# Second block's output projection, layer norms, modulation, residual and tail, token-major in tiles of 128 tokens

## The chip, the cores and the metric

One NeuronCore of a Trainium2 chip (trn2) runs the whole program. Five engines work on their own instruction streams and meet at semaphores: PE multiplies matrices, DVE and ACT work element by element, POOL does small vector work and indirect transfers, SP issues most transfers. The metric is the device time of one execution in microseconds, as the median of several runs.

## The reference

A model of two blocks on 512 tokens of width 1024, float32. The change lies in the second block. Cut to what matters:

```python
def _layernorm(z, gain=None, bias=None):
    mu = mean(z); var = mean(square(z - mu))
    y = (z - mu) * rsqrt(var + 1e-6)
    return y if gain is None else y * gain + bias

def _modulate(z, shift, scale):
    return _layernorm(z) * (1 + scale) + shift

mod = silu(c) @ w_ada + b_ada                      # 6 rows of 1024: sh1 sc1 g1 sh2 sc2 g2
mixed = _mixer(...)                                # mLSTM heads and RWKV heads, 512 + 512 wide
x = _layernorm(ALPHA * x + g1 * (mixed @ w_out), ln1_g, ln1_b)
ffn = _hier_moe(_modulate(x, sh2, sc2), ...)       # 32 experts, 2 chosen for each token
x = _layernorm(ALPHA * x + g2 * ffn, ln2_g, ln2_b) # the output
```

The routing takes logits = h @ rt + bias with h the modulated activation, 36 of them for each token (4 groups, 32 experts), picks a group and two experts in it, and weights their results by `share`.

## The kernel before

Activations lie feature-major: a tensor `[128, 8, 512]` holds feature k*128+p of token t at partition p, chunk k, column t. Weights stream from memory in units of `[128, 2048]` (1 MB, sixteen 128x128 blocks) through a ring of four buffers; `Weights.feed` on SP reloads a buffer when `w.used` says it is free, and the last reloads of a stage already bring the next stage's units.

`rwkv_stage` (L2056) runs the RWKV scan in six steps of 128 tokens in two directions. SP loads the factors F of step p into one of two buffers when step p-2 is through with it (L2126); no other transfer follows the masks of step 0.

`route_stage` (L2696) comes next. `HeadNorm` (L2558) normalises the RWKV heads of the mixer output `o` in place: PE sums, DVE centres, ACT squares, PE sums squares, a reciprocal on DVE, then four `tensor_spread` matmuls that DVE multiplies in, chunk by chunk. Between these PE works ahead on the output projection (`chunk`, L2747): output chunk m of 128 features is one PSUM bank of 512 tokens, eight matmuls with a 128x128 weight block stationary and a chunk of `o` moving; chunks 0 to 4 take their first four k early. DVE then adds the gated product to `x`, which ACT has multiplied by ALPHA (L2818, L2903). Then `Norm` (L2641) runs twice, first with ln1's gain and bias in place, then with the modulation into `h`: eight ones-matmuls give the mean over features to every partition (`sum_chunk`, L2658), DVE subtracts it (L2681), ACT squares (L2671), eight ones-matmuls sum the squares (L2663), DVE, ACT and DVE make the 128x512 rstd (L2684, L2673, L2686), DVE multiplies (L2690) and ACT applies scale and shift (L2676). PE then makes the logits with `rt` stationary (36 rows, 512 columns; L2779), turns them to token-major (L2783), and turns `h` into `tokens_sb`, 128 tokens at a time (L2790, ACT copies L2913), which SP stores to `tokens` in memory (L2736). DVE meanwhile does the routing from L2828 on; PE gives it ranks (L2796, L2799) and the slot table (L2805).

`experts_stage` (L2927) loops over 32 experts: POOL gathers token rows by slot from `tokens`, PE multiplies, POOL scatters results to `pair_rows`; SP feeds the ring. `tail_stage` (L3195) loads the two result rows of each token in four tiles, DVE scales and sums them (L3228, L3230), PE turns each tile to feature-major (L3244), DVE adds gate times it to `x` (L3235), and a third `Norm` runs; each of its eight chunks is stored to `out` as it is placed (L3215).

The order on each engine is written out by hand; stages are blocks with a barrier between them.

## Time and profile before

| | us |
|---|---|
| median of 3 runs (3359.12 to 3368.25) | 3359.33 |
| the profiled execution's own time | 3374.72 |
| its span, first to last instruction | 3372.9 |
| PE busy | 3055.4 (91%) |
| DVE busy | 1942.2 (58%) |
| ACT busy | 1274.9 (38%) |
| POOL busy | 909.9 (27%) |
| mean granted TensorE clock | 0.957 of 2.4 GHz |

Busy times are sums over the span, so an engine with 91% can still leave whole stretches to others; a stretch is read from the windows. A granted clock of 1.0 is 2.4 GHz and 0.5 is 1.2 GHz. A matmul of float32 operands stands in the trace as two records.

### The profile page before, as it was taken

What the parts mean: (1) busy time and instruction counts of PE and PEld (TensorE: products, weight loads), DVE (VectorE), ACT (ScalarE), POOL (GpSimd) and SP (SyncE); (2) the same over time, 40 slices, a digit from 0 to 9 for tenths busy, and PEclk for the clock granted to TensorE, in tenths of its full rate; (3) what the DMA queues carried; (4) which work ended last, traced back from release to release, by engine and by line L of the source; (5) the groups of instructions that cost most, each with busy time, mean ns of one, the idle gap of its engine ahead of it and who ended that gap; (6) DMA issues with size and microseconds to landing.
All of it is one profiled execution on the core that took longest, in us unless ns stands there. A gap on an engine that the chain in (4) does not pass through costs nothing. (4 is left out here: it accounts for less than half of the span.)

```text
span 3372.9 us, 54470 instructions
## 1 busy us (share of the span) xinstructions
PE 3055.4 (91%) x22376; PEld 2398.5 (71%) x22376; DVE 1942.2 (58%) x2706; ACT 1274.9 (38%) x1607; POOL 909.9 (27%) x468
## 2 busy tenths in 40 slices
PE   7989999998999979999989998369999769999995
PEld 5567888797777757888768777257785358888783
DVE  3656552201433335563299837865653469999895
ACT  2544322222333333322232222412222247787773
POOL 3023444333222204344312210000100024454431
PEclk9989999999999989999999998779999979999997
DMA  3633222322111103222221100411102159999994
GB/s 143 231 120 112 95 92 100 132 88 77 61 63 57 57 29 109 89 98 97 104 75 63 50 18 1 149 63 43 39 29 92 38 213 354 362 384 364 361 368 195
DMA packets 77474, 439.69 MB, mean 130 GB/s; under 512 B 14944, under 2 KB 18016, under 8 KB 28512
## 3 DMA queue, kind: packets, MB, share of 16 engines
q1 hardware_dynamic: 67776, 427.38, 34.2%
q0 software_dynamic: 9504, 9.47, 0.8%
q8 instruction: 153, 2.51, 0.3%
q14 instruction: 41, 0.34, 0.0%
HBM read 422.11 MB, written 39.85 MB: 137 GB/s over the span
## 5 line engine op out<-in xcount | busy, mean ns | idle before, releaser
L77 POOL TENSOR_TENSOR ring_lo<-ring,unit_hi 128x2048 fp32r<-128x2048 f32 x116 | 536.6, 4626 | 1124.0 <-ACT unit_hi L72 1124.0
L130 PE MATMUL wide<-h_hi,unit_hi 128*128 128x512 f32 x1296 | 516.0, 398 | 44.8 <-DVE h_lo L191 23.3
L132 PE MATMUL wide<-h_hi,ring_lo 128*128 128x512 f32 x1296 | 516.8, 399 | 0.0
L131 PE MATMUL wide<-h_lo,unit_hi 128*128 128x512 f32 x1296 | 515.7, 398 | 0.0
L3149 DVE TENSOR_TENSOR ex_w_lo<-ring,ex_w_hi 128x2048 fp32r<-128x2048 f32 x192 | 437.7, 2288 | 49.5 <-ACT ex_w_hi L3099 48.8
L3099 ACT CAST ex_w_hi<-ring 128x2048 fp32r<-128x2048 f32 x192 | 365.9, 1908 | 123.3 <-DMA ring<-in_weights 115.6
L72 ACT CAST unit_hi<-ring 128x2048 fp32r<-128x2048 f32 x116 | 220.5, 1901 | 417.8 <-PE wide L132 416.3
L130 PEld LDWEIGHTS wide<-h_hi,unit_hi 128*128 128x128 f32 x1296 | 249.7, 193 | 116.4 <-POOL ring_lo L77 18.8
L131 PEld LDWEIGHTS wide<-h_lo,unit_hi 128*128 128x128 f32 x1296 | 245.7, 190 | 53.6 <-issue 0.2
L132 PEld LDWEIGHTS wide<-h_hi,ring_lo 128*128 128x128 f32 x1296 | 245.1, 189 | 52.4
L362 DVE TENSOR_TENSOR ffn_hidden_lo<-ffn_whole,ffn_hidden_hi 128x512 f32 (+1 forms) x44 | 201.0, 4568 | 51.6 <-ACT ffn_hidden_hi L337 51.6
L3042 PE MATMUL wide<-ex_w_hi,ex_x_hi 128*128 128x512 f32 x512 | 204.9, 400 | 7.5 <-DVE ex_x_lo L3154 6.2
L3044 PE MATMUL wide<-ex_w_hi,ex_x_lo 128*128 128x512 f32 x512 | 201.5, 394 | 0.0
L3043 PE MATMUL wide<-ex_w_lo,ex_x_hi 128*128 128x512 f32 x512 | 201.1, 393 | 0.0
L3001 POOL TENSOR_TENSOR ex_held<-ex_blank 128x1 f32<-128x1 f32 x64 | 90.1, 1407 | 320.8 <-DVE ex_results L3178 319.6
L130 PE MATMUL wide<-in_hi,in_unit_hi 128*128 128x512 f32 (+3 forms) x424 | 148.3, 350 | 16.1 <-DVE in_lo L1207 8.8
L1480 DVE SCALAR_TENSOR_TENSOR conv<-grid,cols,conv 128x512 f32<-128x512 f32 x160 | 158.4, 990 | 3.5
L132 PE MATMUL wide<-in_hi,ring_lo 128*128 128x512 f32 (+3 forms) x424 | 147.1, 347 | 0.0
L2514 ACT COPY rw_Q<-wide 128x256 f32<-128x256 f32 (+1 forms) x144 | 53.5, 371 | 230.6 <-PE wide L2217 189.9
L130 PE MATMUL wide<-ffn_hidden_hi,unit_hi 128*128 128x512 f32 x352 | 140.1, 398 | 0.0
L131 PE MATMUL wide<-ffn_hidden_lo,unit_hi 128*128 128x512 f32 x352 | 139.7, 397 | 0.0
L132 PE MATMUL wide<-ffn_hidden_hi,ring_lo 128*128 128x512 f32 x352 | 138.0, 392 | 0.0
(526 smaller groups left out, 6006.9 us busy)
## 6 DMA issues: line engine op xcount, KB each, us to landing
ring<-in_weights SPq DMA_DIRECT2D x356, 1024.0 KB
factors<-rp_out SPq DMA_DIRECT2D x8, 1536.0 KB, 5.5
rw_F<-factors SPq DMA_DIRECT2D x12, 1024.0 KB
tail_both<-pair_rows_out SPq DMA_DIRECT2D x4, 1024.0 KB, 7.9
x<-in_x SPq DMA_DIRECT2D x1, 2048.0 KB, 7.5
x_kept<-x SPq DMA_DIRECT2D x1, 2048.0 KB, 11.9
x<-x_kept SPq DMA_DIRECT2D x1, 2048.0 KB
x_mixing<-x SPq DMA_DIRECT2D x1, 2048.0 KB, 7.3
```

Source lines behind the costliest of these rows:

```text
L72: act.copy(self.hi[n % 2][:, :], self.ring[n % RING][:, :]).then_inc(self.hi_ready, 1)
L77: pool.tensor_tensor(self.lo[n % RING][:, :], self.ring[n % RING][:, :], self.hi[n % 2][:, :].bitcast(F32), ALU.subtract).then_inc(self.lo ...
L130: pe.matmul(dst, a[0], b[0], start=start, stop=False)
L131: pe.matmul(dst, a[0], b[1], start=False, stop=False)
L132: return pe.matmul(dst, a[1], b[0], start=False, stop=stop)
L362: dve.tensor_tensor(hidden[1][:, j * RING + i, :], whole[:, i % 2, :], hidden[0][:, j * RING + i, :].bitcast(F32), ALU.subtract).then_inc( ...
L1480: dve.scalar_tensor_tensor(out=go, in0=shifted(dy, dx), scalar=weight(dy, dx), in1=go, op0=ALU.mult, op1=ALU.add).then_inc(convolved, 1)
L3042: pe.matmul(dst, a_hi, b_hi, start=first, stop=False)
L3043: pe.matmul(dst, a_hi, b_lo, start=False, stop=False)
L3044: return pe.matmul(dst, a_lo, b_hi, start=False, stop=last)
L3099: act.copy(w_hi[at % RING][:, :], w.ring[n % RING][:, :]).then_inc(hi_ready, 1)
L3149: dve.tensor_tensor(w_lo[at % RING][:, :], w.ring[n % RING][:, :], w_hi[at % RING][:, :].bitcast(F32), ALU.subtract).then_inc(w.used, 1)
```

## The change

- The weight units of `w_out` are laid out by row chunk, so unit n holds k = 2n and 2n+1 for all 1024 outputs. A tile of the projection is 128 tokens by 1024 features in two banks: `o`'s 128x128 block is stationary and 512 weight columns move.
- `x` (feature-major, from memory) is turned on PE in eight rounds of four transposes through bank 5; ACT multiplies by ALPHA on the way into `normed`.
- Gate, gains, biases, scale and shift are needed along the free dimension. Four modulation vectors are stored to `mod_rows` in memory during `rwkv_stage` (step 2, SP), and they and `ln_rows` are loaded into all 128 partitions: five in `route_stage`, three at the start of `experts_stage`.
- `Norm` is replaced by `RowNorm`: for each tile of 128 tokens two `bn_stats`, one `bn_aggr`, and the norm as two `scalar_tensor_tensor` around a square root and a reciprocal of one column.
- The modulated tile is already what goes to `tokens`; it is turned (eight transposes, two ACT copies) only for the logits, which come out token-major with the bias added on DVE.
- The tail works on the tiles as they are loaded and stores four tiles; ACT takes over the first product with `share`. PE has nothing to do there.

The diff's core:

```diff
 rwkv_stage, sync:
+                    if p == 2:
+                        for to, of in stores:
+                            sp.dma_start(to, of, allow_slow_non_contiguous=True).then_inc(rows_stored, 16)
+                sp.wait_ge(rows_stored, 16 * len(stores))
...
+class RowNorm:
+    def vector(self, dve, n, src, mid, dst, scale, shift):
+        for i in range(2):
+            self.step(dve.bn_stats(self.parts[:, i, :], src[:, i * T:(i + 1) * T]), i == 1)
+        dve.bn_aggr(self.stats[:, n, :], self.parts[:, :, :].rearrange("p i s -> p (i s)")).then_inc(self.measured, 1)
+        dve.wait_ge(self.measured, n + 1)
+        dve.scalar_tensor_tensor(out=mid, in0=src, scalar=self.stats[:, n, 0:1], in1=scale, op0=ALU.subtract, op1=ALU.mult)
+        dve.wait_ge(self.root_ready, n + 1)
+        self.step(dve.reciprocal(self.rstd[:, n:n + 1], self.rstd[:, n:n + 1]))
+        return dve.scalar_tensor_tensor(out=dst, in0=mid, scalar=self.rstd[:, n:n + 1], in1=shift, op0=ALU.mult, op1=ALU.add)
+    def scalar(self, act, n):
+        act.wait_ge(self.measured, n + 1)
+        act.activation(self.rstd[:, n:n + 1], self.stats[:, n, 1:2], ACT.Sqrt, bias=self.eps[:, 0:1]).then_inc(self.root_ready, 1)
...
 route_stage, sync:
-                for n in range(RING):
+                for n in range(2):
                     w.load(sp, w.at + n)
                 sp.dma_start(x[:, :, :], kept).then_inc(head.x_back, 16)
+                for n in range(2, RING):
+                    w.load(sp, w.at + n)
...
 route_stage, tensor:
+                def tile(t, halves, first_k, last_k):
+                    for k in range(first_k, last_k):
+                        if k >= MC:
+                            pe.wait_ge(head.mixed_ready, k - MC + 1)
+                        unit = w.arrived(pe, 0, k // 2)
+                        for half in halves:
+                            b = k % 2 * D + half * T
+                            mm = pe.matmul(c.bank[2 * t + half][:, :], o[:, k, t * P:(t + 1) * P], unit[:, b:b + T], start=(k == 0), stop=(k == DC - 1))
+                        if t == TT - 1 and k % 2 == 1:
+                            mm.then_inc(w.used, 1)
+                    return mm
                 head.tensor_sums(pe)
-                chunk(0, 0, MC)
+                tile(0, (0, 1), 0, MC)
                 head.tensor_squares(pe)
-                chunk(1, 0, MC)
-                chunk(2, 0, MC)
+                tile(1, (0, 1), 0, MC)
                 head.tensor_spread(pe, 0)
                 head.tensor_spread(pe, 1)
-                chunk(3, 0, MC)
+                for n in range(4):
+                    turn_x(n // 2, n % 2)
                 head.tensor_spread(pe, 2)
                 head.tensor_spread(pe, 3)
...
+                for n in range(4, 2 * TT):
+                    turn_x(n // 2, n % 2)
+                tile(2, (0,), 0, MC)
+                for t in range(2):
+                    tile(t, (0, 1), MC, DC).then_inc(tile_done, 1)
+                tile(2, (0,), MC, DC)
+                pe.wait_ge(x_grown, 2 * TT)
+                tile(2, (1,), 0, DC).then_inc(tile_done, 1)
+                pe.wait_ge(head.scaled, MC)
+                tile(3, (0, 1), 0, DC)
+                turn_h(0)
+                turn_h(1)
+                logits_of(0)
+                turn_h(2)
+                logits_of(1)
+                logits_of(2)
+                turn_h(3)
+                logits_of(3)
...
 route_stage, vector, for each tile t:
+                    for half in range(2):
+                        cols = slice(half * T, (half + 1) * T)
+                        dve.tensor_tensor(h[:, t, cols], c.bank[2 * t + half], rows.gate[:, cols], ALU.mult).then_inc(gated, 1)
+                    dve.tensor_tensor(normed[:, t, :], normed[:, t, :], h[:, t, :], ALU.add).then_inc(added, 1)
+                    norm.vector(dve, 2 * t, normed[:, t, :], normed[:, t, :], normed[:, t, :], rows.scale1, rows.shift1).then_inc(normed_ready, 1)
+                    norm.vector(dve, 2 * t + 1, normed[:, t, :], h[:, t, :], h[:, t, :], rows.scale2, rows.shift2).then_inc(tokens_ready, 1)
...
 experts_stage, sync:
+                for to, of in rows_of:
+                    sp.dma_start(to, of).then_inc(rows_loaded, 16)
...
 tail_stage, scalar:
+                for t in range(TT):
+                    act.wait_ge(loaded[t], 16)
+                    act.mul(both[:, t, 0, :], both[:, t, 0, :], route.share[:, t, 0:1]).then_inc(scaled, 1)
+                    norm.scalar(act, t)
 tail_stage, vector, for each tile t (waits left out):
+                    dve.scalar_tensor_tensor(out=y, in0=both[:, t, 1, :], scalar=route.share[:, t, 1:2], in1=y, op0=ALU.mult, op1=ALU.add).then_inc(summed, 1)
+                    dve.tensor_tensor(y, y, rows.gate, ALU.mult).then_inc(gated, 1)
+                    dve.tensor_tensor(x[:, t, :], x[:, t, :], y, ALU.add).then_inc(added, 1)
+                    norm.vector(dve, t, x[:, t, :], x[:, t, :], x[:, t, :], rows.scale, rows.shift).then_inc(placed, 1)
...
+                stores = [(mod_rows[n].rearrange("(k p) -> p k", p=P), source[:, part * DC:(part + 1) * DC, 0])
+                          for n, source, part in ((GATE1, mod, 2), (SHIFT2, mod, 3), (SCALE2, mod1, 4), (GATE2, mod, 5))]
```

## Rows read from the trace of the kernel before

**Rows 1.** Windows: us, busy and (count) of PE, PEld, DVE, ACT, POOL, granted clock, DMA share, GB/s
```profile
2643.00:2668.00 25.00, 17.15 (x32) 6.34 (x32) 13.83 (x18) 11.39 (x17) 0.00 (x0) 0.86 0.08 34
2668.00:2696.00 28.00, 19.12 (x46) 6.03 (x45) 14.88 (x21) 12.68 (x18) 0.00 (x0) 0.88 0.00 1
2696.00:2719.00 23.00, 13.22 (x75) 11.04 (x73) 14.45 (x74) 4.23 (x7) 0.00 (x0) 0.78 0.23 91
2719.00:2731.00 12.00, 0.82 (x4) 0.82 (x5) 4.49 (x2) 5.01 (x4) 9.54 (x17) 0.52 0.64 232
2731.00:3325.00 594.00, 575.98 (x2686) 474.93 (x2684) 520.33 (x318) 437.24 (x318) 253.64 (x242) 0.98 0.93 350
3325.00:3372.90 47.90, 23.42 (x64) 12.22 (x64) 27.33 (x34) 16.93 (x26) 0.00 (x0) 0.71 0.33 132
```

**Rows 2.** Timeline, norm stretch: start us, us, engine, line, out<-in, idle before
```profile
2643.46 4.88 DVE L2681 SCALAR_TENSOR_TENSOR x<-wide,x 128x512 f32<-128x512 f32 x8 [1.82 <-PE wide L2658]
...
2653.99 3.35 DVE L2686 RECIPROCAL norm_rstd<-norm_rstd 128x512 f32<-128x512 f32 x1 [0.70 <-ACT norm_rstd L2673]
...
2695.73 0.31 DVE L2828 COPY rt_L<-wide 128x144 f32<-128x144 f32 x1 [1.17 <-PE wide L2783]
```

**Rows 3.** Timeline, PE in the output projection
```profile
2575.03 5.40 PE L2747 MATMUL wide<-late,ring 128*128 128x512 f32 x8 [2.13 <-DMA ring<-in_weights]
...
2595.20 13.90 PE L2747 MATMUL wide<-late,ring 128*128 128x512 f32 x32
```

**Rows 4.** Timeline, PE's first token transposes
```profile
2695.62 1.97 PE L2790 MATMUL wide<-ident,h 128*128 128x128 f32 x16
```

**Rows 5.** Groups by shape, DVE: line, names, shapes, count | busy us, mean ns | idle before
```profile
L1943 DVE TENSOR_TENSOR_SCAN rp_cum<-rp_reset,rp_sg 128x768 f32<-128x768 f32 x4 | 7.0, 1757 | 2.8 <-ACT rp_up L1891 1.9 <-ACT rp_sg L1876 0.9
...
L3230 DVE SCALAR_TENSOR_TENSOR tail_both<-tail_both,share 128x1024 f32<-128x1024 f32 x4 | 5.1, 1284 | 0.1
...
L3228 DVE TENSOR_SCALAR tail_both<-tail_both,share 128x1024 f32<-128x1024 f32 x4 | 3.0, 754 | 13.8 <-DMA tail_both<-pair_rows_out 13.8
...
L1707 DVE RECIPROCAL ml_small<-ml_small 128x4 f32<-128x4 f32 x16 | 2.9, 178 | 0.6
...
L2619 DVE TENSOR_TENSOR late<-late,wide 128x512 f32<-128x512 f32 x4 | 2.7, 684 | 2.3 <-PE wide L2599 2.3
...
L2880 DVE TENSOR_TENSOR rt_at_high<-iota,rt_high 128x1024 f32<-128x1024 f32 x1 | 1.2, 1225 | 0.0
...
L2606 DVE COPY hn_heads<-ident 128x512 f32<-128x512 f32 x1 | 0.4, 418 | 0.0
```

**Rows 6.** Groups by shape, ACT
```profile
L2527 ACT COPY rw_base<-wide 128x512 f32<-128x512 f32 x1 | 0.6, 586 | 0.2 <-PE wide L2288 0.2
```

**Rows 7.** Timeline, tail: first product, last transposes, DVE's first read, stores
```profile
3330.63 0.75 DVE L3228 TENSOR_SCALAR tail_both<-tail_both,share 128x1024 f32<-128x1024 f32 x1 [12.60 <-DMA tail_both<-pair_rows_out]
...
3340.18 1.97 PE L3244 MATMUL wide<-ident,tail_both 128*128 128x128 f32 x8 [0.50 <-DVE tail_both L3230]
3340.70 5.36 DVE L3235 SCALAR_TENSOR_TENSOR x<-wide,mod,x 128x512 f32<-128x512 f32 x8 [0.57 <-PE wide L3244]
...
3365.62 5.26 SPq L3215 DMA_DIRECT2D out<-x  x8
```

**Rows 8.** Windows, PE just after the second norm's sums may start
```profile
2658.00:2664.00 6.00, 5.03 (x6) 2.19 (x7) 4.29 (x8) 5.75 (x8) 0.00 (x0) 0.50 0.00 0
```

**Rows 9.** F loads on SP, their first matmuls by line, page's part 3
```profile
2304.95 0.32 SPq L2126 DMA_DIRECT2D rw_F<-factors  x1
...
2356.33 2.49 SPq L2126 DMA_DIRECT2D rw_F<-factors  x2
...
L2180 PE MATMUL wide<-rw_F x64: 212/218/268, 2363.5 to 2367.6; 64*64 64x64 f32 x64
...
q1 hardware_dynamic: 67776, 427.38, 34.2%
q0 software_dynamic: 9504, 9.47, 0.8%
```

More of the change, by code:

```diff
@@ L2693, with route_stage @@
 NOBODY = 1 << 20
-def route_stage(nc, c, w, o, x, kept, g, bonus, gate, first, second, h, consts, loads, route, tokens):
+def route_stage(nc, c, w, o, x, kept, g, bonus, rows, hT, consts, loads, route, tokens):
     NR = E_GROUPS + EXPERTS
@@ new lines, in logits_of @@
+                def logits_of(t):
+                    if t == 0:
+                        pe.wait_ge(gated, 2 * 2)
+                        pe.wait_ge(loaded, 16 * len(loads))
+                    for k in range(DC):
+                        if k % 4 == 0:
+                            pe.wait_ge(h_copied, 2 * t + k // 4 + 1)
+                        mm = pe.matmul(logits[:, t * NR:(t + 1) * NR], hT[:, t % 2, k, :], rt[:, k, :], start=(k == 0), stop=(k == DC - 1))
+                    mm.then_inc(logits_done, 1)
@@ L2762, in _ @@
-                for m in range(DC):
-                    chunk(m, MC if m < head.EARLY else 0, DC)
-                    if m >= 2:
-                        pe.wait_ge(added, m - 1)
-                        first.sum_chunk(pe, m - 2)
-                for k in range(DC - 2, DC):
-                    pe.wait_ge(added, k + 1)
-                    first.sum_chunk(pe, k)
-                first.sum_squares(pe)
-                for k in range(DC):
-                    pe.wait_ge(first.placed, k + 1)
-                    second.sum_chunk(pe, k)
@@ L2775, in _ @@
-                second.sum_squares(pe)
-                pe.wait_ge(loaded, 16 * len(loads))
-                for k in range(DC):
-                    pe.wait_ge(second.placed, k + 1)
-                    mm = pe.matmul(logits, rt[:, k, :], h[:, k, :], start=(k == 0), stop=(k == DC - 1))
-                mm.then_inc(logits_done, 1)
-                pe.wait_ge(logits_copied, 1)
-                for t in range(TT):
-                    mm = pe.matmul(small[:, t * NR:(t + 1) * NR], LT[:, t * P:(t + 1) * P], c.ident[0:NR, 0:NR], start=True, stop=True)
@@ L2811, in _ @@
                 head.vector(dve)
-                for m in range(DC):
-                    if m % 2 == 0:
-                        dve.wait_ge(chunk_done, m // 2 + 1)
-                    else:
-                        dve.wait_ge(w.used, w.at + m // 2 + 1)
-                    dve.wait_ge(grown, m + 1)
-                    dve.scalar_tensor_tensor(out=x[:, m, :], in0=c.bank[m][:, :], scalar=gate(m), in1=x[:, m, :],
-                                             op0=ALU.mult, op1=ALU.add).then_inc(added, 1)
@@ L3192, in experts_stage, with tail_stage @@
     w.at += ALL
-def tail_stage(nc, c, route, pair_rows, x, gate, scale, shift, out):
+def tail_stage(nc, c, route, pair_rows, rows, rows_loaded, out):
     with ExitStack() as ctx:
@@ L3224, in _ @@
             @block.vector
             def _(dve):
+                norm.begin(dve)
                 for t in range(TT):
[L3227 to L3228 removed]
+                    y = both[:, t, 0, :]
                     dve.wait_ge(scaled, t + 1)
[L3230 to L3231 removed]
@@ L3368, in second_block @@
-            second = Norm(c, x, dev, h, at(4, 0, True), at(3), c.bank[2], c.bank[3], squares, rstd[:, 1, :])
-            loads = [(rt[:, :, :], a["rt"]), (rt_bias[:, :], a["rt_bias"]), (iota[:, :], a["iota"]), (earlier[:, :], a["earlier"]),
-                     (pairs[:, :, :, :], a["pairs"])]
-            route_stage(nc, c, w, mixed, x, kept, r.g, r.bonus, at(2), first, second, h, (rt, rt_bias, iota, earlier, pairs), loads, route, tokens)
-        experts_stage(nc, c, w, route, tokens, pair_rows)
+            hT, rows = late[:, 8192:8192 + 2 * D].rearrange("p (i k t) -> p i k t", i=2, t=P), Bag()
@@ new lines, in second_block @@
+            route_stage(nc, c, w, mixed, x, kept, r.g, r.bonus, rows, hT, (rt, rt_bias, iota, earlier, pairs), loads, route, tokens)
+        rows, rows_loaded = Bag(), nc.alloc_semaphore("tail_rows_loaded")
+        rows.gate, rows.scale, rows.shift = [sb(f"tail_row_{n}", [P, D])[:, :] for n in ("g2", "ln2_g", "ln2_b")]
+        rows_of = [(rows.gate, mod_rows[GATE2].partition_broadcast(P)), (rows.scale, a["ln_rows"][2].partition_broadcast(P)),
+                   (rows.shift, a["ln_rows"][3].partition_broadcast(P))]
```

251 lines of the change are left out of this document (114 added, 137 removed).

## The prediction

> **What bounds the kernel now.** I read the stretches first [rows 1]. The expert stretch, 594 of 3372.9 us, keeps the DMA queues busy 0.93 of the time at 350 GB/s; the change touches nothing in it. What it touches lies in two places where one engine after another works alone. From 2643 to 2696 us the two layer norms run feature-major over the whole 1024 x 512 activation: PE is busy 17.15 of 25 us and 19.12 of 28 us, DVE and ACT 11 to 15 us each. The timeline shows the relay [rows 2]: centring may start only when all eight chunk sums are in (2643.46), the rstd needs all eight squares, the reciprocal of a 128x512 tile costs 3.35 us (2653.99), the second norm repeats all of it, and the logits and their turn follow. So 52.3 us pass between the first centring (2643.46) and the first routing instruction on the copied logits (L2828, 2695.73). The tail, 3325 to 3372.9, is the same relay once more, with PE at clock 0.71. Routing itself (2696 to 2719) is small DVE instructions, which stay.
>
> **Part 1: PE up to the first finished tile.** The projection is 64 f32 matmuls of 512 moving columns in either layout. Sixteen took 13.90 us (32 records), so 0.86 to 0.87 each [rows 3]; token-major swaps which operand is stationary and keeps count and columns. I take no gain or loss. The start is as before: the first unit lands at 2575.03 and the first four matmuls take 5.40 us there. Now eight stand before the head norm's squares: 5.4 + 4 x 0.86 = 8.9, to 2583.9. Squares (1.0) and tile 1's eight (6.9) go to 2591.8, two spreads to 2593.5. Then come the added turns of x: eight rounds of four transposes on PE and one ACT multiply into SBUF, through a single bank, so a relay. Sixteen transposes took 1.97 us [rows 4], 0.12 each; DVE's first read in the tail began 0.52 us after its transposes did [rows 7]; an ACT copy of 128x512 out of PSUM is 0.59 [rows 6]. One round is 0.52 + 3 x 0.12 + 0.59 + 0.05 = 1.5 us, eight are 12.2, and two more spreads stand between them (1.7): 2607.4. Twelve matmuls follow before tile 0 is whole (half of tile 2's first four chunks, then tile 0's last four): 10.3, so 2617.7. After a stretch in which PE had idled and then worked in bits, the granted clock was 0.50 [rows 8]; the turns are such bits. All turns at half rate would add 3 us and the first matmuls behind them 2.5. I add 0.8, giving 2618.5, and keep 0 and 5.5 as ends.
>
> **Part 2: DVE per tile, route stage.** Now DVE carries both norms alone, tile by tile. Prices are from [rows 5]: two gate products out of PSUM, 0.684 each, 1.37; residual add, 128x1024, 1.225. One norm: two bn_stats of 128x512, one aggregate on 12 values (0.18, as small ones take), two scalar_tensor_tensor of 128x1024 at 1.284, a reciprocal of one column 0.178. No bn_stats is in this trace. As a one-pass instruction it costs about what a tensor_tensor of that width does, 0.684; that is my value, being an elementwise read with no second operand. Its lower end is the SBUF copy, 0.418; its upper end the scan's two cycles an element, 1757 ns for 768, so 1.17. The norm is then 1.37 + 0.18 + 2.57 + 0.18 = 4.30. A tile is 1.37 + 1.23 + 8.60 + 0.4 for some fourteen gaps of 0.03 = 11.6 us, and four are 46.4. ACT's square root of one column (about 0.2 us) lies under the scalar_tensor_tensor of 1.284 that stands between it and its reader. PE needs 6.9, 10.3 and 13.8 us for tiles 1, 2 and 3, together 31.0, while DVE works 34.8 on three tiles: DVE waits only for tile 0, and PE has 3.8 us of cover. DVE ends at 2618.5 + 46.4 = 2664.9. Behind the last tile stand eight transposes (the clock low by then, 0.246 each), a pair of ACT copies of which one is exposed, and the last four small logits matmuls: 1.3 + 1.0 + 0.6 + 1.2, to 2669.0 against 2695.73. That is 26.7 us. Removed with it: LT's copy, the logits' transposes, the token transposes and their copies; the last two lay beside routing and give nothing. But they kept PE at work just ahead of the rank matmuls. These and the sixteen records of L2805 will find a low clock; routing ran at 0.78 on average [rows 1], and going to 0.5 on about 6 us of its matmuls costs about 1.5. Route: 25.2 us.
>
> **Part 3: queues.** On SP, x is asked for behind two units instead of four and the loads grow by five rows spread over 128 partitions, 2.5 MB. In all 9 MB from 2569 at 350 to 430 GB/s are in by 2595, and the first reader is DVE at 2618: covered by 23 us. The refill with expert weights, which waited for the early chunks, now waits for tile 3 (2635 to 2648); 4 MB land by 2660, and the experts start about 2693: covered. The token stores stand behind these waits on SP and are needed only then. In the RWKV stage SP gets four stores whose elements are 4 bytes: 4096 packets, issued about 2305.3, behind one tile's F loads and ahead of the next F load (2356.33) on the same queue; that tile's first matmul starts at 2363.5 [rows 9], about when its 2 MB are in, so there is no lead to spend. Nothing in the trace writes 4-byte pieces to memory from a tile. The software queue's packets, of 1 KB in the mean, took 0.8% of 16 x 3372.9 over 9504, 0.045 us each; all of q1's took 0.27. So the stores are through after 12 us, or after 69. I take the low value, since 4 bytes are nearer to 1 KB than to q1's 6.3, and count nothing. The experts' queue gets 1.5 MB of rows before its first weight: 4 us at 350 GB/s in a stretch that used the DMA 0.64 [rows 1], sharing with the gather PE waits for. I count 0.7 lost; 0 to 4 are the ends.
>
> The Trainium skill (DMA: Bandwidth & Descriptors, Rules for kernel authors) says that a strided last dim is lowered to one descriptor per element and should be made contiguous; the same page puts read-modify-write under 512 B. It speaks against these stores. By it the packets are slow, and the sum would lose what rival C loses; no row here shows a 4-byte store.
>
> **Part 4: tail.** Tile 0's pair rows are in at 3330.63 [rows 7]. ACT scales them (1.0, from 0.586 for half the width, less one start [rows 6]), a product DVE had made in 0.754 [rows 5]; DVE then does 1.284 (sum), 1.225 (gate), 1.225 (add) and a norm of 4.30, with gaps 8.35. Four are 33.4: 3331.6 + 33.4 = 3365.0. ACT's next scaling (1.0) runs beside the last two DVE steps. The loads came every 2.5 us and are no longer the bound. The last store is 512 KB instead of 256 KB; the last one was issued at about 3370.6 and the span ended 2.3 later, so I give 3.1: 3368.1. Gain 4.8 us. Gone are 16 ones-matmuls, 32 transposes and the 3.35 reciprocal.
>
> **The sum.** 25.2 + 4.8 - 0.7 = 29.3. The profiled execution's own time was 3374.7 (span 3372.9), so 3345.4 there. The runs' median was 3359.3, 15.4 lower than that execution; the shortened parts do not depend on it, so 3359.3 - 29.3 = 3330.0.
>
> **Rivals.**
> (B) bn_stats takes two cycles an element, like the scan: 24 x (1.17 - 0.684) = 11.7 us back, 3341.7. For: it keeps a mean and a variance. Against: nothing chained to the previous element has to be waited for.
> (B2) bn_stats streams at the SBUF copy's rate, 24 x 0.27 = 6.4 more: 3323.6. DVE's three tiles then take 31.6 us, still over PE's 31.0, so all of it shows. VectorE: DVE Perf Modes of the Trainium skill (Mode 2x_2P) has single-source f32 operations in SBUF at two elements a cycle; the trace agrees for tensor_scalar, 754 against 1284 ns [rows 5], but the page leaves open which operations have it.
> (C) The 4-byte stores hold the queue. With q1's mean of 0.27 us a packet they last 69 us from 2305.3, to 2374.4, so F for the next tile starts 18 us late and PE stands as long: 3348.
> (D) The same, slower than before. If a packet takes t us, the stores end at 2305.3 + 256 t, and PE waits 256 t - 51. It equals my gain at t = 0.31. At 0.35 us it is 38.6 against 29.3: 3368.6. For: single elements and a destination in memory. Against: t would be over q1's mean, whose packets hold 427.38 MB / 67776 = 6.3 KB, where q0's of 1 KB took 0.045.
> (E) The norms gain, but PE with its turns and low clock becomes the bound instead of DVE: the full 5.5 us where 0.8 is counted, and another 3.5 at tile 3, 8.2 in all: 3338.
>
> **How the numbers follow.** Forecast (3325 to 3336) 0.58, B 0.12, B2 0.07, C 0.06, D 0.06, E 0.11. The predicted time is the forecast's, 3330.0. The range 3316 to 3348 takes in B, B2, E and the nearer half of C; left out are D, the rest of C, and of the others the part that their own spread puts beyond it, together under 0.2. A change of 0.3% is 10 us, about what a measurement of this kernel can tell from none. Faster: forecast, B, B2 and E, 0.88, less 0.01 for several losses at once: 0.87. Same: C, which at 3348 stands on the edge of 0.3%, and that 0.01: 0.07. Slower: D, 0.06.
>
> **What would show it.** The bn_stats row near 0.68 us; DVE's tiles 11.6 us apart with no wait for PE after the first; first gate product at 2618; logits added at 2669; DVE in the tail 8.35 a tile, out stores at intervals; 4096 4-byte packets over well before 2356, and no long PE wait on rw_F. Wrong would be a PE wait on rw_F of tens of us, a bn_stats over 1.2, or gate products waiting for tile 1 or 2.

## The result and the profile after

| | us |
|---|---|
| median of the changed kernel, 4 runs (3327.13 to 3332.01) | 3330.0 |
| median of the kernel before beside it, 4 runs (3359.12 to 3370.02) | 3363.79 |
| ratio, with its 95% interval | 0.9892 (0.9875 to 0.9909) |
| span of the profiled execution, before | 3372.9 |
| span of the profiled execution, after | 3327.9 |

The time came out at 3330.0 us, the forecast's own figure. That is less of a success than it looks: the stretches below show two terms of 9 and 17 us, of opposite sign, that the forecast had at zero. First the page of the changed kernel, its busy times and two of its DMA queues; q1 has 4880 packets more than before for 4.2 MB more [rows 9].

```profile
PE 2990.6 (90%) x22320; PEld 2383.9 (72%) x22320; DVE 1954.2 (59%) x2725; ACT 1250.8 (38%) x1572; POOL 898.5 (27%) x468
...
q1 hardware_dynamic: 72656, 431.59, 35.1%
...
q8 instruction: 153, 2.51, 0.3%
```

Windows of the kernel after, columns as in [rows 1]. In order: route stage to the first gate product; to the last token row finished; to the logits added; routing; experts up to PE's first transposes; the rest of the experts; the tail.

```profile
2561.10:2606.60 45.50, 39.45 (x113) 17.69 (x114) 17.74 (x25) 10.37 (x17) 0.00 (x0) 0.96 0.52 203
2606.60:2650.70 44.10, 39.04 (x144) 21.65 (x142) 42.84 (x60) 5.37 (x14) 0.00 (x0) 0.95 0.38 132
2650.70:2656.30 5.60, 5.42 (x24) 5.06 (x24) 0.09 (x2) 2.45 (x3) 0.00 (x0) 0.50 0.23 94
2656.30:2682.80 26.50, 12.92 (x44) 11.16 (x44) 14.69 (x74) 0.52 (x3) 0.00 (x0) 0.55 0.00 0
2682.80:2696.80 14.00, 0.00 (x0) 0.00 (x0) 4.53 (x3) 5.09 (x4) 10.76 (x19) 0.53 0.95 334
2696.80:3286.00 589.20, 572.63 (x2688) 474.39 (x2688) 520.42 (x318) 437.94 (x319) 243.59 (x240) 0.99 0.94 353
3286.00:3327.90 41.90, 0.00 (x0) 0.00 (x0) 31.28 (x37) 10.60 (x13) 0.00 (x0) 0.50 0.38 151
```

DVE is busy 42.84 of the 44.10 us in which the four tiles are made: it is the bound there, where before [rows 1, 2] three engines took turns. One tile on DVE's timeline; the first row's 11.53 us is the only wait for PE's products, and the next tile begins at 2617.61 with none:

```profile
2606.59 1.29 DVE L2838 TENSOR_TENSOR tokens_sb<-wide,row_g 128x512 f32<-128x512 f32 x2 [11.53 <-PE wide L2737]
...
2607.91 1.22 DVE L2841 TENSOR_TENSOR y<-y,tokens_sb 128x1024 f32<-128x1024 f32 x1
...
2609.17 1.29 DVE L2663 BATCH_NORM_STATS2 rt_norm_parts<-y 128x6 f32<-128x512 f32 x2
...
2610.49 0.21 DVE L2664 BATCH_NORM_AGGREGATE rt_norm_stats<-rt_norm_parts 128x2 f32<-128x12 f32 x1
...
2610.73 1.29 DVE L2666 SCALAR_TENSOR_TENSOR y<-y,rt_norm_stats,row_ln_g 128x1024 f32<-128x1024 f32 x1
...
2616.41 1.29 DVE L2669 SCALAR_TENSOR_TENSOR tokens_sb<-tokens_sb,rt_norm_rstd,row_sh 128x1024 f32<-128x1024 f32 x1
...
2617.61 1.28 DVE L2838 TENSOR_TENSOR tokens_sb<-wide,row_g 128x512 f32<-128x512 f32 x2
```

PE over the same stage: the products ahead of the squares, the turns of x as a relay with ACT (1.34 us a round), the 96 records behind them without a gap, and the last tile's logits and the slots with the clock at 0.50 to 0.55.

```profile
2566.89 8.83 PE L2737 MATMUL wide<-ring,late 128*128 128x512 f32 x16 [1.86 <-DMA ring<-in_weights]
...
2586.62 0.66 PE L2752 MATMUL wide<-ident,x 128*128 128x128 f32 x4 [0.69 <-ACT y L2924]
2587.96 0.66 PE L2752 MATMUL wide<-ident,x 128*128 128x128 f32 x4 [0.69 <-ACT y L2924]
...
2595.98 41.37 PE L2737 MATMUL wide<-ring,late 128*128 128x512 f32 x96
...
2652.59 3.63 PE L2776 MATMUL wide<-rt,late 128*128 128x36 f32 x16
...
2674.15 6.74 PE L2822 MATMUL wide<-rt_named,rt_at_low 128*128 128x256 f32 x16 [5.86 <-DVE rt_named L2905]
2696.81 1.97 PE L3072 MATMUL wide<-ident,tokens_sb 128*128 128x128 f32 x8 [15.93 <-DMA tokens_sb<-tokens,ex_take]
```

**Where the time went.** The program falls into stretches by the start of one instruction each: the first load of RWKV factors (L2126), SP's first instruction of the route stage, of the experts, of the tail. The difference of the two spans is 45.0 us, and these are all of it:

| stretch | before | after | difference | forecast |
|---|---|---|---|---|
| all up to the first RWKV factors | 2191.7 | 2175.0 | -16.7 | 0 |
| RWKV stage | 377.3 | 386.1 | +8.8 | 0 |
| route stage | 149.9 | 121.7 | -28.2 | -25.2 |
| experts (of it up to PE's first transposes) | 606.9 (11.3) | 603.2 (14.0) | -3.7 (+2.7) | +0.7 |
| tail | 47.1 | 41.9 | -5.2 | -4.8 |

The execution of before that was profiled took 3374.7 us, 11 over its median, and that of after 3329.7, which is its median; so 34 us is what runs show, and the table's parts are 11 us richer than that. No instruction of the first row's stretch was changed. The experiments are about that row and the second.

### The profile page after: what moved, and what is told of

Same layout as the page of the kernel before. It is cut to its first block and busy times, and to the rows that moved or that the text cites. A ratio compares the mean times of both kernels' runs of the same rounds, so it can differ in the third digit from the quotient of the medians.

```text
span 3327.9 us, 54357 instructions
## 1 busy us (share of the span) xinstructions
PE 2990.6 (90%) x22320; PEld 2383.9 (72%) x22320; DVE 1954.2 (59%) x2725; ACT 1250.8 (38%) x1572; POOL 898.5 (27%) x468
## 3 DMA queue, kind: packets, MB, share of 16 engines
q8 instruction: 153, 2.51, 0.3%
## 5 line engine op out<-in xcount | busy, mean ns | idle before, releaser
L130 PE MATMUL wide<-h_hi,unit_hi 128*128 128x512 f32 x1296 | 516.1, 398 | 44.9 <-DVE h_lo L191 23.0
L132 PE MATMUL wide<-h_hi,ring_lo 128*128 128x512 f32 x1296 | 508.1, 392 | 0.0
L131 PE MATMUL wide<-h_lo,unit_hi 128*128 128x512 f32 x1296 | 507.9, 392 | 0.0
L130 PEld LDWEIGHTS wide<-h_hi,unit_hi 128*128 128x128 f32 x1296 | 245.2, 189 | 110.6 <-POOL ring_lo L77 18.8
L130 PE MATMUL wide<-in_hi,in_unit_hi 128*128 128x512 f32 (+3 forms) x424 | 149.5, 353 | 15.0 <-DVE in_lo L1207 8.0
L130 PE MATMUL wide<-ffn_hidden_hi,unit_hi 128*128 128x512 f32 x352 | 139.1, 395 | 0.0
```

The lines of the kernel that those rows point to most:

```text
L130: pe.matmul(dst, a[0], b[0], start=start, stop=False)
L131: pe.matmul(dst, a[0], b[1], start=False, stop=False)
L132: return pe.matmul(dst, a[1], b[0], start=False, stop=stop)
```

## The experiments

Of each kernel one execution was profiled. Stretches as in the table above; "gate" is route start to the first gate product, "logits" from there to the logits added, "routing" from there to the experts. The first row is the kernel before, unedited; its medians are those of the four sets of its runs that stood beside the others.

| kernel | median us (runs) | ratio to before, 95% | up to RWKV | RWKV | gate | logits | routing | first transposes | experts | tail |
|---|---|---|---|---|---|---|---|---|---|---|
| before | 3363.79 to 3366.93 | 1 | 2191.7 | 377.3 | 33.3 | 93.4 | 23.2 | 11.3 | 606.9 | 47.1 |
| after_again | 3332.24 (4) | 0.9896 (0.9864 to 0.9929) | 2179.4 | 384.3 | 43.7 | 49.8 | 25.6 | 13.2 | 606.5 | 42.0 |
| bn_twice | 3344.67 (7) | 0.9937 (0.9918 to 0.9956) | 2169.8 | 381.4 | 45.5 | 59.2 | 24.9 | 13.2 | 603.8 | 46.5 |
| before_no_recip | 3355.36 (10) | 0.9973 (0.9958 to 0.9988) | 2190.0 | 371.7 | 31.1 | 87.4 | 23.1 | 11.5 | 606.2 | 45.3 |
| tile0_first | 3326.73 (4) | 0.9886 (0.9864 to 0.9909) | 2176.8 | 380.5 | 41.9 | 50.9 | 25.3 | 14.5 | 609.4 | 42.1 |
| warm_route | 3326.10 (4) | 0.9889 (0.9868 to 0.9909) | 2171.9 | 381.2 | 45.4 | 48.4 | 23.0 | 14.5 | 610.9 | 42.0 |
| rows_at_end | 3326.49 (4) | 0.9883 (0.9848 to 0.9917) | 2177.1 | 382.1 | 43.6 | 49.7 | 26.0 | 11.3 | 606.7 | 42.1 |
| no_stores | 3906.40 (4) | 1.1604 (1.1567 to 1.1641) | 2174.4 | 369.9 | 47.2 | 49.7 | 26.0 | 14.0 | 1195.9 | 42.1 |
| stores_x5 | 3369.24 (10) | 1.0006 (0.9994 to 1.0018) | 2179.1 | 421.7 | 47.3 | 49.7 | 25.8 | 14.9 | 606.4 | 42.2 |
| rows_by_pe | 3320.31 (4) | 0.9857 (0.9836 to 0.9877) | 2176.9 | 372.8 | 46.7 | 49.7 | 25.8 | 13.5 | 611.5 | 41.9 |
| cols_padded | 3344.41 (4) | 0.9927 (0.9908 to 0.9946) | 2195.2 | 385.9 | 43.4 | 49.7 | 25.9 | 13.5 | 609.5 | 42.0 |
| before_narrow | 3349.34 (6) | 0.9945 (0.9927 to 0.9963) | 2175.5 | 373.2 | 31.5 | 92.7 | 23.0 | 11.3 | 610.3 | 47.0 |
| best | 3311.94 (4) | 0.9843 (0.9827 to 0.9859) | 2170.6 | 376.0 | 40.8 | 48.8 | 20.5 | 14.1 | 609.1 | 42.2 |

**after_again**: the changed kernel once more, unedited.

> The changed kernel itself, unaltered, for what its stages do from run to run. Theory 1 (the added RWKV time of its profile, 386 us against 377, is the clock's own wandering): the stretch from the first F load to the first out-projection weight load comes out between 377 and 386 and the granted clock in step 2 of it differs from the first profile's 0.84. Theory 2 (the 4-byte stores bring the clock down): again about 386 with a clock near 0.84 in step 2. Route stage 121 to 122 us, tail 42 us in either.

3332.24 us. It shows how far one kernel's stretches vary from execution to execution: 4.4 us up to RWKV, 1.8 at the gate, 3.3 in the experts.

### Is DVE's tile the bound, and what does the norm cost?

**bn_twice**: every bn_stats is issued twice, the first into a spare tile.

```
+ self.step(dve.bn_stats(self.parts2[:, n, i, :], src[:, i * T:(i + 1) * T]), False)
  self.step(dve.bn_stats(self.parts[:, i, :], src[:, i * T:(i + 1) * T]), i == 1)
```

> Every bn_stats issued twice, the first into a tile nobody reads. Theory 1 (DVE is the bound of both places and PE stays covered): 24 more at about 0.65 us each add 15.5 us in all, 10.3 in the route stage and 5.2 in the tail. Theory 2 (PE or the relay of waits is the bound in the route stage): under 5 us more there, 5.2 in the tail.

The groups of DVE by shape in this kernel, the real ones and the added ones of the route stage:

```profile
L2664 DVE BATCH_NORM_STATS2 rt_norm_parts<-y 128x6 f32<-128x512 f32 x16 | 11.0, 686 | 0.3
L2665 DVE BATCH_NORM_STATS2 rt_norm_parts<-y 128x6 f32<-128x512 f32 x16 | 10.8, 676 | 0.0
```

Sixteen added instructions of 0.676 us are 10.8 us; the stretch "logits" grew by 9.5 (49.7 to 59.2). Eight in the tail are 5.4; the tail grew by 4.5. Nearly all of what DVE is given shows up in the time, in both stages: DVE is the bound, and an instruction saved there is worth its duration.

**before_no_recip**: the kernel before with the reciprocal of the 128x512 tile (3.35 us [rows 2]) replaced by a copy; the three norms leave out the reciprocal, so their outputs are others.

```
- dve.reciprocal(self.rstd, self.rstd).then_inc(self.rstd_ready, 1)
+ dve.tensor_copy(self.rstd, self.rstd).then_inc(self.rstd_ready, 1)
```

> The kernel before, in which the three layer norms copy the 128x512 root instead of taking its reciprocal (the reciprocal is left out, so the output is not the reference's). Theory (the norms of before are a relay and every instruction of it is on the path): 3 x (3.35 - 0.42) = 8.8 us less than before. Rival (another engine's work fills in): under 3 us less.

In the route the two norms gave back 6.0 us (93.4 to 87.4) where two times 3.35 - 0.43 are 5.8, the tail 1.8 of 2.9. So the reciprocals are some 8 of the 33 us that route and tail gained; the other 25 lie in the rest of the relay, which the token-major form ends as well.

### The route's smaller terms

**tile0_first**: the third tile's first products no longer stand ahead of the first two tiles' last ones.

```
- tile(2, (0,), 0, MC)
  for t in range(2):
      tile(t, (0, 1), MC, DC).then_inc(tile_done, 1)
- tile(2, (0,), MC, DC)
+ tile(2, (0,), 0, DC)
```

> The four early matmuls of tile 2 stand behind tiles 0 and 1 instead of ahead of tile 0's last ones. PE's total is unchanged. Theory (DVE bound with 2.45 us of cover for PE at tile 3): first gate product 3.4 us earlier, DVE then waits about 1.1 us for PE at tile 3, and the route stage is 2.3 us shorter. Rival (PE is as much a bound): DVE waits more at tiles 2 or 3, and the stage is 0 to 1 us shorter.

The first gate product came 41.9 us after the route's start in place of 43.7 and 45.5 (43.4 to 47.3 in the nine profiles with the old order), and 1.1 to 1.2 of that was lost again behind it, where DVE now waits once more for PE's products (1.1 us). The route is 118.1 us against 119.1 and 121.7; the median, 3326.73, cannot be told from that of after.

**warm_route**: four matmuls without use ahead of the last tile's transposes, six behind its logits and ahead of the wait for the ranks' input, six behind the ranks.

```
+ warm(4)          # four times pe.matmul(c.bank[3], c.ones, o[:, 0, :])
  turn_h(3)
  logits_of(3)
+ warm(6)
  ...
  mm.then_inc(ranks_done, 1)
+ warm(6)
```

> Adds 16 matmuls whose result nobody reads, in three gaps of PE: four before the last tile's transposes, six before the ranks, six before the slot table. Theory (the route's end lost time because PE stood idle and its granted clock fell to 0.53 there): the clock in that stretch above 0.8, last logits 3.6 to under 2.5, ranks 6.3 to 3.5, slot table 6.7 to 3.5 us, and the route stage 5 to 8 us shorter. Rival (the added matmuls end too late or the rate is set by other things): gain under 2 us or a loss of up to 3.

"Logits" 48.4 in place of 49.7, routing 23.0 in place of 25.6 and 26.5: 4 to 5 us of what the low clock of the two windows after 2650.7 above costs; it was still 0.85 in this kernel's routing. The total moved by less than its spread.

**rows_at_end**: the tail's rows are asked for behind the last expert weight, not ahead of the first.

```
- for to, of in rows_of:                      # ahead of the ring
-     sp.dma_start(to, of).then_inc(rows_loaded, 16)
  ... all of the experts' weights ...
+ for to, of in rows_of:
+     sp.dma_start(to, of).then_inc(rows_loaded, 16)
```

> The three rows for the tail are loaded behind the experts' last weight unit instead of ahead of the first. Theory 1 (they delayed the first gather, for which PE waits): from the experts' first DVE instruction to PE's first transpose 11.3 us instead of 14.0, and the whole 2.7 us shorter. Rival (the stage is bound by the weight transfers, so the gather's delay is made up): 11.3 us likewise, the total the same as the changed kernel.

PE's first transposes come after 11.3 us, as before the change, in place of 13.2 and 14.0: those 2 to 3 us are the rows. But the expert stretch as a whole takes 606.7, with 606.5 and 603.2 where the start is late. Over all profiles but that of no_stores it is 606.2 to 610.3 us (mean 607.5) in the four that start early, and 603.2 to 611.5 (607.8) in the nine that start late. That fits a stretch in which the DMA, at 0.93 of its time, sets the end and a late first expert is made up; but 2 us would not stand out of this spread, so it is not shown. Nor does the median tell: 3326.49 is 3.5 and 5.8 us under the two of after, and the single times overlap.

### The four stores

**no_stores**: the four stores left out, and other rows of the same size loaded where their results were read. The modulation is then another, the tokens fall to the experts otherwise, and the loop over the experts runs twice; only its stretches ahead of the experts are read.

```
- rwkv_stage(..., stores)
+ rwkv_stage(..., [])
- (rows.gate, mod_rows[GATE1].partition_broadcast(P))
+ (rows.gate, a["ln_rows"][0].partition_broadcast(P))
```

> Leaves out the four 4-byte stores of the modulation vectors; gate, scale and shift rows are loaded from the layer-norm rows instead, so the output is not the reference's. Theory 1 (stores cost nothing): same total as the changed kernel within 0.1%, RWKV stretch anywhere in 377 to 386. Theory 2 (the stores slow the RWKV stage through the clock or the queue): RWKV stretch back to 377 in the profile and the total 6 to 9 us lower than the changed kernel.

**stores_x5**: the four stores and sixteen more like them into a tensor that nothing reads.

```
+ stores += [(extra_rows[4 * i + n].rearrange("(k p) -> p k", p=P), of) for i in range(4) for n, (to, of) in enumerate(stores[:4])]
```

> The same four 4-byte stores and sixteen more like them into other memory rows, 20480 packets in place of 4096. The forecast's mechanism (a queue before the next F load, free while it is short): the four took about 15 us from their issue, so twenty take about 75 and end 12 to 21 us after the next F load was due; PE waits on rw_F by that much and the total is 3342 to 3351 us. Rival (packets of 4 bytes pass beside other loads): no added PE wait on rw_F, total as the changed kernel's.

No stores: the RWKV stage takes 369.9 us. Five times the stores: 421.7, and 37 us on the median, all of the change's gain and more than either theory gave it. In both PE waits 36 us for rw_F, as in after (36.8): it is the first load's landing, and the factors behind the stores are never late. So the queue that the forecast looked at is not what makes it slow. Windows of 10 us around the stores; in after they are issued from 2287.26 on. First after, then no_stores, then 40 us of stores_x5 (the DMA share goes over 1 there because the records of small packets overlap):

```profile
2285.00:2295.00 10.00, 6.94 (x226) 6.34 (x226) 4.58 (x12) 1.12 (x3) 0.00 (x0) 0.81 0.72 204
2295.00:2305.00 10.00, 5.10 (x88) 4.24 (x89) 1.43 (x4) 0.37 (x1) 0.00 (x0) 0.50 0.21 2
2305.00:2315.00 10.00, 9.43 (x189) 7.05 (x191) 5.52 (x13) 1.12 (x3) 0.95 (x3) 0.67 0.01 2
```

```profile
2285.00:2295.00 10.00, 7.02 (x280) 6.26 (x275) 4.49 (x12) 1.86 (x5) 0.00 (x0) 1.00 0.60 214
2295.00:2305.00 10.00, 9.21 (x306) 7.38 (x307) 8.32 (x19) 1.49 (x4) 1.58 (x4) 1.00 0.02 5
2305.00:2315.00 10.00, 9.87 (x183) 7.35 (x181) 9.71 (x20) 1.84 (x5) 2.74 (x6) 1.00 0.01 2
```

```profile
2298.00:2338.00 40.00, 28.95 (x438) 21.77 (x435) 12.30 (x28) 2.23 (x6) 1.72 (x5) 0.54 1.15 3
```

In the ten microseconds from 2295 all engines do little in after (PE 88 matmuls in place of 306, DVE 4 instructions in place of 19), and the clock is 0.50 where it stays at 1.00 without the stores. What DVE waits for, in after, and last what L2416 waits for in the whole stage (us, times, longest):

```profile
2293.00 0.44 DVE L2416 COPY_PREDICATED rw_X<-level_mask,wide 128x256 f32<-128x256 uint32 x1 [0.23 <-PE wide L2246]
...
2302.24 0.45 DVE L2416 COPY_PREDICATED rw_X<-level_mask,wide 128x256 f32<-128x256 uint32 x1 [8.47 <-remote]
...
DVE rw_X L2416 <- PE wide L2246: 119.0, 78, 4.6
```

"Remote" is the profile's word for a signal that it can put down to no instruction just before it. The semaphore that L2416 waits for is raised by PE's matmuls of L2246; here that was at 2302.22, 2.8 us after the last record of those matmuls. So DVE's input was late, and the late engine is PE. PE stands three times between 2294.0 and 2301.6 (1.6, 1.1 and 1.7 us) for nothing that the profile shows. ACT has such a wait of 8.1 us, on PE's L2221. In stores_x5 DVE has ten of them, 40.2 us together, up to 10.6, all on PE. In tile0_first PE stands 7.94 us at a stretch. The same 30 us of the stage, from 110 us behind its first load, in before and in after:

```profile
2301.70:2331.70 30.00, 26.87 (x768) 22.23 (x766) 21.56 (x50) 4.81 (x13) 3.43 (x9) 0.94 0.20 73
```

```profile
2285.00:2315.00 30.00, 21.48 (x499) 17.63 (x501) 11.53 (x29) 2.60 (x7) 0.95 (x3) 0.66 0.31 69
```

PE is busy 19.0 to 21.8 us of these 30 in all eight kernels with the 4-byte pieces, and 25.8 to 26.9 in all six without. The clock has a part in it, but it is not where it begins: in after it falls to 0.50 at 2291.2, behind a PE wait of 1.7 us and ahead of the long ones. In before it falls at nearly the same point of the stage (118 us in for 116) and is back after 3.4 us; in after it stays low for 20.5. In tile0_first it is 0.89 in the mean of these 30 us, and PE is busy for only 19.0.

Now the DMA view from 2292 to 2304 of after and of no_stores: GB/s in 40 slices of 0.3 us, in which a 55 is one packet of q8, and the queues.

```profile
GB/s 3 1 1 0 0 0 55 0 0 0 0 0 0 0 0 3 5 2 1 1 4 5 2 2 1 1 0 0 0 0 0 0 0 55 0 0 0 0 0 0
...
q1 hardware_dynamic: 2463, 0.01, 22.2%
q8 instruction: 2, 0.03, 2.4%
```

```profile
GB/s 27 27 0 0 55 0 0 0 0 0 0 0 0 0 0 0 55 0 0 0 0 0 0 0 0 0 0 55 0 0 0 0 0 0 0 0 0 0 0 0
...
q8 instruction: 3, 0.05, 1.7%
```

The instructions of the engines come in by a queue too, q8, in packets of 16 KB, one every 3.3 to 3.6 us in no_stores. The profile counts its packets on the same 16 DMA engines as the 2463 of 4 bytes. In after one comes at 2293.8 and the next only at 2301.9. The packets of q8 also take longer there: 2.4% of 16 x 12 us over two is 2.3 us each, where 1.7% over three is 1.1 in no_stores. My reading is that PE ran short of instructions behind the small packets, that the others waited for it, and that its clock stayed at 1.2 GHz meanwhile. The Trainium skill (Advanced Engine Details and Errata, ISA Cache) gives an engine's instruction cache lines of 16 KB, 256 instructions; the trace agrees in the size, 2.51 MB over 153 packets of q8. This stays a reading: no run forced it. For it speaks tile0_first, where one packet of q8 took 6.5 us, from 2295.9 to 2302.5, and PE stood from 2295.7 to 2303.65. Against it speaks bn_twice, where no packet of q8 beside or behind the stores took over 1.51 us and the stage is 381.4 us all the same. A rival was not tested: the small packets may hold up something else, such as the signals of PE, which came 2.8 us behind its records.

**rows_by_pe**: PE turns the four rows (four transposes of 128x8) at the start of the RWKV stage, where it waits for the first factors anyway; ACT copies them, and one DMA stores 32 pieces of 512 bytes.

```
+ for n, of in enumerate(stores[1:]):
+     mm = pe.transpose(c.bank[2][0:DC, n * P:(n + 1) * P], of, c.ident[:, :])
+ act.copy(rowsT, c.bank[2][0:DC, :].rearrange("k (n p) -> k n p", p=P)).then_inc(rows_copied, 1)
  if p == 0:
+     sp.dma_start(stores[0], rowsT).then_inc(rows_stored, 16)    # in place of the four at p == 2
```

> The kernel after, with the four rows of modulation turned by four transposes of 128x8 on TensorE at the start of the RWKV stage, where it waits some 35 us for the first factors, copied by ScalarE and stored by one DMA in pieces of 512 bytes, in place of four DMAs with 4096 pieces of 4 bytes. Theory S, the small pieces hold up the DMA engines on which the engines' instructions come in too, VectorE or ScalarE stands 8 to 10 us with nothing to wait for, and TensorE comes back at the low clock: the RWKV stretch is 370 to 377 us long, as in the kernels with no stores (369.9, 371.7, 377.3), in place of 380.5 to 386.1, no such wait of 8 us is left, and the median is 3332.2 - 9.6 = 3322.6 us. Theory T, the stretch varies with something other than the size of the pieces: it stays at 380 or over, and the median at 3332 us.

The RWKV stage is 372.8 us, no wait of 8 us is left there, and DVE and PE go on around 2295, the clock at 0.91 and 0.92:

```profile
2285.00:2295.00 10.00, 7.47 (x264) 6.94 (x264) 4.36 (x12) 1.49 (x4) 0.00 (x0) 0.91 0.57 213
2295.00:2305.00 10.00, 9.21 (x302) 7.62 (x296) 7.25 (x18) 1.49 (x4) 0.79 (x2) 0.92 0.02 3
```

The median is 3320.31, 9.7 to 11.9 below the two of after, though the intervals of the ratios still touch. Over all profiles the stage takes 380.5 to 386.1 us in the seven with the four stores (mean 383.1) and 369.9 to 377.3 in the six without 4-byte pieces (373.5): 9.6 us. This kernel changes the size of the pieces, their number and their place at once, and no run put large pieces at the old place. With stores_x5, where only the number grew, and no_stores it leaves little doubt that the 4-byte pieces in step 2 cost this time; by what way is the open reading above.

### The stretch that nobody changed

The change takes the two norms' gains and shifts out of `c.cols`, the tile of per-feature columns. It is 256 columns wide in place of 288, so every SBUF tile allocated behind it, x and the first block's operands among them, lies 128 bytes per partition lower.

**cols_padded**: after, with 32 unused columns.

```
- ("r_norm_w", MC), ("r_norm_b", MC)])
+ ("r_norm_w", MC), ("r_norm_b", MC), ("unused", 4 * DC)])
```

> The kernel after with 32 unused columns put back at the end of the tile of per-feature columns, so that this tile is again 288 columns wide and every SBUF tile allocated behind it lies 128 bytes per partition higher, as in the kernel before; no instruction is added or taken away. In the profiles so far the first load of RWKV factors is issued 2169.8 to 2179.4 us after the start in all eight kernels with the narrow tile and at 2190.0 and 2191.7 us in the two with the wide one. Theory A, the addresses do it: that load is issued at about 2190 us and the median is 3332.2 + 14 = 3346 us. Theory B, something else in the program does it (its length, where the code of each engine lies): the load stays near 2175 us and the median at 3332 us.

**before_narrow**: before, with those 32 columns in a tile of their own at the top of SBUF.

```
- ("ln1_g", DC), ("ln1_b", DC), ("ln2_g", DC), ("ln2_b", DC)])
+ ])
+ ln_cols = nc.alloc_sbuf_tensor_at("ln_cols", [P, 4 * DC], F32, offset=kept_at + 4 * (DC * T + TT * D + 2 * P))
```

> The kernel before with the gains and shifts of its two layer norms (32 columns) in a tile of their own at the top of SBUF, loaded in the route stage, so that the tile of columns is 256 wide and the tiles behind it lie 128 bytes lower, as in the kernel after. Theory A, addresses: the first load of RWKV factors is issued near 2175 us in place of 2190 to 2192, and the median is 3364.7 - 14 = 3351 us. Theory B, something else: near 2191 us, and 3364 to 3366 us.

Each went where the address says. Padding put the start of the RWKV stage back to 2195.2 and cost 12 to 14 us of median; narrowing brought it to 2175.5 in the kernel before and gave 17.6 us (3366.93 to 3349.34) with nothing else of the change in it. Over all profiles that start is 2169.8 to 2179.4 in eleven with the narrow tile and 2190.0 to 2195.2 in three with the wide one. Part of it shows in the first block's second feed-forward, 1300 to 1540 us: PE's groups by line in before, cols_padded, after, before_narrow.

```profile
L132 PE MATMUL wide<-h_hi,ring_lo 128*128 128x512 f32 x340 | 135.0, 397 | 0.0
L131 PE MATMUL wide<-h_lo,unit_hi 128*128 128x512 f32 x340 | 134.6, 396 | 0.0
```

```profile
L132 PE MATMUL wide<-h_hi,ring_lo 128*128 128x512 f32 x339 | 134.9, 398 | 0.0
L131 PE MATMUL wide<-h_lo,unit_hi 128*128 128x512 f32 x339 | 134.9, 398 | 0.0
```

```profile
L132 PE MATMUL wide<-h_hi,ring_lo 128*128 128x512 f32 x348 | 135.5, 389 | 0.0
L131 PE MATMUL wide<-h_lo,unit_hi 128*128 128x512 f32 x348 | 135.5, 389 | 0.0
```

```profile
L131 PE MATMUL wide<-h_lo,unit_hi 128*128 128x512 f32 x350 | 136.2, 389 | 0.0
L132 PE MATMUL wide<-h_hi,ring_lo 128*128 128x512 f32 x350 | 136.1, 389 | 0.0
```

The same matmuls take 389 ns in the mean in the two kernels with the narrow tile and 397 in the two with the wide one, at clock 1.00 or 0.99 in all four. Only the two groups that read `h_lo` or `ring_lo` differ: the third, L130 on `h_hi` and `unit_hi`, takes 389 to 391 ns in all four. Which tile has to lie where, and why 8 ns hang on it, stays open: no run moved one tile alone.

### All together

**best**: rows_by_pe with the edits of tile0_first and warm_route.

> The rows by TensorE as in the run before, with the two edits of the route that each took 2 to 5 us off it: all of the third tile's products behind the first two tiles, and a few unused matmuls ahead of the last logits and of the slots to keep the clock up. If the terms add: 3322.6 - 3 - 3 = 3317 us, the RWKV stretch 370 to 377 us, and the route 114 to 117 us. If the route's gains overlap: 3320 us. Under theory T of the run before: 3326 us.

3311.94 us, the fastest of all: 1.6% under before, 18 to 20 us under after. The route takes 110.1 us. Its three parts, by windows:

```profile
2546.60:2587.40 40.80, 34.35 (x105) 15.62 (x106) 17.75 (x25) 10.37 (x17) 0.00 (x0) 1.00 0.58 227
2587.40:2636.20 48.80, 48.56 (x185) 27.21 (x184) 43.01 (x62) 7.72 (x17) 0.00 (x0) 1.00 0.37 129
2636.20:2656.70 20.50, 17.34 (x68) 10.20 (x66) 14.65 (x73) 0.46 (x3) 0.00 (x0) 1.00 0.00 0
```

Routing is 20.50 us at clock 1.00 against 26.50 at 0.55 in after, with DVE's work the same 14.65 and 14.69: 6 us were the clock.

## Why the prediction was right, and where it was not

**What bounds it, Parts 1 and 2: held.** The two norms were a relay, and with both of them on DVE tile by tile DVE became the bound. bn_stats took 686 ns where 0.684 was assumed, bn_aggr 0.21 for 0.18; B (1.17 us) and B2 (0.418) fell with it. No form of single-source speed-up shows here: 686 ns is what a tensor_tensor of that width takes [rows 5]. A tile took 11.02 us, not 11.6: I had added fourteen gaps of 0.03, but only some rows have one, and others start before the row ahead of them has ended (2616.41 + 1.29 against 2617.61). Four took 44.1 for 46.4.

**Part 1's size: 4 us too high.** 45.5 us from the route's start for 49.5. Of the turns of x a round took 1.34 us for 1.5, and the last round of each four costs PE only its transposes, ACT's multiply lying beside what follows, so that eight cost 8.9 and not 12.2; and the clock stayed at 1.00 through them, from 2571.1 to 2646.2, so the 0.8 was not needed. E's condition, a low clock behind the turns, did not arise.

**Behind the last tile: 3.3 us too low.** Last transposes to logits added took 5.6 us for 4.1, since the clock was at 0.50 and all eight of the tile's logits matmuls (sixteen records, 3.63 us) lay behind the turn, where I had four of them. Routing lost 3.3 us to the clock (23.2 to 26.5) where 1.5 was given: I costed the ranks and slots and took half. warm_route and best took 3 to 6 us of routing away again. In all the route gained 28.2 in one profile and 30.8 in the other, for 25.2.

**Part 3, experts: the cost stays open.** The rows delay the first expert by 2 to 3 us, inside my ends of 0 and 4 and above the 0.7. But rows_at_end, without that delay, is no shorter in the stage, and the stage varies by 8 us over the profiles: a cost of 0 fits, and so does 0.7.

**Part 3, the stores: the step that failed.** "So the stores are through after 12 us, or after 69 ... and count nothing". The duration was right: the first is issued at 2287.26, and the 4096th 4-byte packet starts at 2299.6, 12.3 us later. C and D fell too, as PE's wait for rw_F did not move. The step asked only who stands behind the stores on SP's queue, and put everything else at nothing. What the runs show in its place is 9.6 us of the stage; around the stores PE is busy 19 to 22 us of 30 in place of 26 to 27. How the pieces do that is not shown. The likeliest way is q8, the queue of instructions, on the same DMA engines; a row of the page shows it, and I had read past it. The Trainium skill (DMA: Bandwidth & Descriptors, Rules for kernel authors) asks for a contiguous last dim in place of one descriptor per element; rows_by_pe, which follows it, measures what that was worth here. I had weighed it as a price on the queue alone.

**Part 4, tail: held.** 7.99 us a tile for 8.35, a gain of 5.2 for 4.8. The last DVE instructions, from which the last store follows:

```profile
3322.22 1.29 DVE L2666 SCALAR_TENSOR_TENSOR y<-y,tail_norm_stats,tail_row_ln_g 128x1024 f32<-128x1024 f32 x1
3323.42 0.16 DVE L2668 RECIPROCAL tail_norm_rstd<-tail_norm_rstd 128x1 f32<-128x1 f32 x1
3323.61 1.28 DVE L2669 SCALAR_TENSOR_TENSOR y<-y,tail_norm_rstd,tail_row_ln_b 128x1024 f32<-128x1024 f32 x1
```

**What the sum had no term for.** The 17 us of the narrower tile. The diff shows it, as four names struck out of a list of columns; I read it as a table that shrinks. Two runs show that the addresses do it, cols_padded and before_narrow; by what mechanism stays open.

**How 3330.0 came about.** The sum gave 29.3 us off a median of 3359.33. Runs beside the kernel after gave 33.8 (3363.79 - 3330.0), and 32.5 beside after_again. Route and tail brought 31 to 36 us for 30.0 (the route is 149.9 us in before's profile but 147.2 in before_narrow's, which has the same instructions there), the stores took 9.6, the address brought 12 to 18. At the lower ends these make the 33 that runs show. The mechanism that was forecast is there at nearly its forecast size; that the total met the number so closely is luck: it comes from two errors of opposite sign, which leave 2 to 8 us, and from a median of before that stood 4 to 8 us under the later ones.

## What to carry to other kernels

Price a transfer by all that it can hold up, and not only by what stands behind it on its queue: 4096 pieces of 4 bytes were through in 12 to 14 us, made no load late, and still cost 9.6 us. The queue of the engines' own instructions, which the profile counts on the same DMA engines, is the first thing to look at there. When an edit changes the size of an early SBUF tile, pad it to the old size in one run, so that the move of all later tiles is not booked as the edit's gain or loss. And where per-token statistics run feature-major through matmuls of ones, turning the tiles token-major lets one engine do a norm at a stretch; from then on each of its instructions is worth nearly its full duration (9.5 of 10.8 us here).

## What the runs showed of the hardware that was not expected

- 4096 stored pieces of 4 bytes lengthened the stage around them by 9.6 us, and 20480 by 48 (421.7 - 373.5), with the factors that PE waited for on time in both. Single waits of DVE or ACT for PE were up to 8.5 us long in after and 10.6 in stores_x5, and PE stood 7.9 us at a stretch in tile0_first.
- Moving SBUF tiles by 128 bytes per partition changed f32 matmuls of the first block from 397 to 389 ns and the whole program by 12 to 18 us.
- The granted clock was 1.00 while PE made the projection. It fell to 0.50 at 2646.2, while PE was at the third tile's logits behind a wait of 1.2 us, and before the 4.0 us in which PE stood ahead of the last tile's transposes (2646.8 to 2650.8). It stayed at 0.55 through a routing in which PE was busy 12.9 of 26.5 us. With sixteen unused matmuls of 512 columns in best it was 1.00 in all of it.
